# Order of the three products in the split FFN matmuls of a two-block transformer kernel

## The chip, the cores and the metric

One Trainium2 chip, one core of it. The metric is the device time of one execution in microseconds (us), the median of three runs. Engines are named as in the profile: PE is TensorE's matmuls and PEld its weight loads, DVE is VectorE, ACT is ScalarE, POOL is GpSimd, and SP issues most of the DMAs.

## The reference, cut to what matters

The reference runs a hybrid layer and then a two-layer block on 256 tokens of width 1024 (the second block has 256 context tokens beside them). There are five feed-forward networks (FFNs) in it, all of this form, with the inner width 2816:

```
gt, up = jnp.split(h @ w_ffn_in, 2, axis=-1)      # h: [tokens, 1024]; gt and up: [tokens, 2816]
y = (jax.nn.silu(gt) * up) @ w_ffn_out            # [tokens, 1024]
```

The first and the last FFN (numbers 0 and 4 here) work on 256 tokens, the three in between (1 to 3) on 512.

## The kernel before, in words

Weights come from HBM in chunks of up to 2 MB (`wf`) through a ring of three slots. Everything runs in float32, but the FFN matmuls are made from a split: each operand is written as a high part, rounded to a narrower float type (`fp32r`), and a low part, the difference. A product is then the sum of three matmuls: high weight by high activation, high weight by low activation, low weight by high activation. All three add to the same PSUM tile.

An FFN is cut into 34 halves (half a weight chunk each), in three groups of hidden tiles (8, 8 and 6, the table `GROUPS`). In a group come first 8, 8 or 6 "in" halves: each makes two PSUM tiles (gate and up, `c` = 0 and 1) over 8 contraction slices (`k`). Then come 4 "out" halves, each of which makes two tiles of the output over the group's 8, 8 or 6 slices. So a half has 2 x 8 x 3 = 48 matmuls, or 36 in the out halves of the last group, and an FFN has 1584. Moving operands are 256 or 512 columns wide, as the tokens are.

What each engine does for a half `h`:

- ACT, `w_hi(h + 2)` (line 1258), rounds the weights of a later half to `W_hi`; it waits until half `h - 1` has filled its tiles, as there are three buffers. Then it takes silu of the gate tile.
- DVE, `w_lo(h + 2)` (line 1563), subtracts, which makes `W_lo`. Then it multiplies the up tile into silu (line 1672), or adds an out tile to the residual (line 1656).
- POOL, `ffn_parts`, rounds the product to the high activation (line 630, signal `a_hi`) and then makes its low part (line 632, signal `a_lo`).
- In front of an FFN stands a norm: per slice, DVE scales (line 1591), ACT and POOL modulate, ACT makes the high part `z_hi` (line 1296, signal `norm_hi`), DVE the low part `z_lo` (line 1606, signal `norm_lo`). `z_lo` lies in the tensor `zT_r`; all other operands of the split lie in `arena_r`.

PE issues in program order, in `ffn`: lines 801, 802 and 803 are the three products of one slice and tile. It waits for `W_lo` of the half at the half's start. In the first half of an FFN (`i == 0`) the two tiles alternate slice by slice, and slice `k` waits for `norm_lo` of that slice. In the first out half of a group (`second and j == 0`), slice `k` of the first tile waits for `a_lo` of that slice. Every other half runs tile by tile with no wait per slice.

Of the kernel before, what the change touches and what calls it, by code (L numbers as in the profile page):

```python
# [19 lines left out]
P = 128  # L20
# [6 lines left out]
FT = FF // P  # L27
GROUPS = ((0, 8), (8, 8), (16, 6))
# [290 lines left out]
def build(nc, d, out_x):  # L319
# [5 lines left out]
    with ctx:  # L325
# [72 lines left out]
        def sig(name):  # L398
            if name not in sems:
                sems[name] = ctx.enter_context(nc.semaphore(name))  # L400
            return sems[name]
# [126 lines left out]
        def norm_hi_before(q):  # L528
            return KT * sum(1 for p in SPLIT if p < q)
# [145 lines left out]
        def _(pe):  # L675
            mm = nc.tensor.matmul
# [104 lines left out]
            def ffn(f, nt, q):  # L781

                hi, lo = a_parts(nt)
                zh = z_hi(nt)
                for i, (g, j, second) in enumerate(HALVES):
                    h = FFN_HALVES * f + i
                    nk = GROUPS[g][1] if second else KT
                    wh = W_hi[h % NSPLIT][:, 0:nk * 256].rearrange("p (k n) -> p k n", k=nk)
                    wl = W_lo[h % NSPLIT][:, 0:nk * 256].rearrange("p (k n) -> p k n", k=nk)
                    pe.wait_ge(sig("w_lo"), h + 1)  # L790
                    xh, xl = (hi, lo) if second else (zh, z_lo)
                    b = [open_tile(half_first_tile(h) + c) for c in range(2)]

                    for c, k in ([(c, k) for k in range(nk) for c in range(2)] if i == 0 else
                                 [(c, k) for c in range(2) for k in range(nk)]):
                        if i == 0 and c == 0:
                            pe.wait_ge(sig("norm_lo"), norm_hi_before(q) + k + 1)
                        if second and j == 0 and c == 0:
                            pe.wait_ge(sig("a_lo"), FT * f + GROUPS[g][0] + k + 1)
                        whc, wlc = wh[:, k, c * P:(c + 1) * P], wl[:, k, c * P:(c + 1) * P]  # L800
                        mm(b[c][:, 0:nt], whc, xh[:, k, 0:nt], start=(k == 0), stop=False)  # L801
                        mm(b[c][:, 0:nt], whc, xl[:, k, 0:nt], start=False, stop=False)  # L802
                        last = mm(b[c][:, 0:nt], wlc, xh[:, k, 0:nt], start=False, stop=(k == nk - 1))  # L803
                        if k == nk - 1:
                            last.then_inc(filled, 1)

            def merge(br, y, ready):
                for c in range(4):
# [31 lines left out]
            b = open_tile(TILE["strip"])  # L840
            mm(b[0:16, 0:384], K_tbl[0:33, :], oh[0:33, :], start=True, stop=True).then_inc(filled, 1)
            oh = C("oh_fwd")
            b = open_tile(TILE["cbias"])
            for t in range(2):
                for c in range(CMP_N):
                    at = P * t - 16 * c - 31 + 271
                    col = (t * CMP_N + c) * 16
                    last = mm(b[:, col:col + 16], oh[0:33, at:at + P], K_tbl[0:33, :], start=True, stop=True)
# [3 lines left out]
            for k in range(KT):  # L852
                pe.wait_ge(sig("lru_xc"), k + 1)
                for g in range(2):
                    n = TILE["lru_gates"] + 2 * k + g
                    b = open_tile(n)
# [5 lines left out]
            b = open_tile(TILE["gla_lr"])  # L862
            for k in range(KT):
                last = mm(b[0:16, 0:S], wsm[:, k, 48:64], zT[:, k, 0:S], start=(k == 0), stop=(k == KT - 1))
            last.then_inc(filled, 1)
            wait_evac(pe, TILE["gla_lr"])
            for h in range(4):
                b = open_tile(TILE["gla_al"] + h)
# [14 lines left out]
            for t in range(2):  # L883
                b = open_tile(TILE["gla_t"] + t)
                for h in range(4):
                    last = nc.tensor.transpose(b[:, h * P:(h + 1) * P], C_e[:, h, t * P:(t + 1) * P], C("ident"))
                last.then_inc(filled, 1)
            for t in range(2):
                b = open_tile(TILE["gla_att"] + t)
                for h in range(4):  # L890
                    last = mm(b[:, h * P:(h + 1) * P], C_k[:, h, t * P:(t + 1) * P], C_q[:, h, t * P:(t + 1) * P],
                              start=True, stop=True)
# [24 lines left out]
            for h in range(4):  # L917
                for e in range(2):
                    n = TILE["gla_o"] + 2 * h + e
                    b = open_tile(n)  # L920
# [238 lines left out]
            for jp in range(4):  # L1159
                b = open_tile(TILE["ev_mix"] + jp)  # L1160
                for a in range(2):
                    g = 2 * jp + a
# [1049 lines left out]
```

## Time and profile before

| | us |
|---|---|
| median of three runs | 2772.85 |
| lowest and highest | 2766.75, 2776.7 |
| span of the profiled execution | 2777.6 |
| PE busy, in the span | 2601.2 |
| PEld busy | 2035.4 |
| DVE busy | 1053.4 |
| ACT busy | 715.2 |
| POOL busy | 245.8 |

The profiled execution is one of its own; the trace gives its span from the first to the last instruction and no other time for it. It lies 4.75 us (0.17%) above the median of the timed runs. Matmuls overlap in the records, so the duration of one is longer than the distance from its start to the next one's; that distance is what a matmul costs.

### The profile page before, as it was taken

To read this page: it belongs to the slowest core of one execution; us is meant where nothing else is said; L and a number is where in the kernel's file an instruction comes from. 1 tells how busy PE (TensorE), PEld (TensorE's weight loads), DVE (VectorE), ACT (ScalarE), POOL (GpSimd) and SP (SyncE) were. 2 spreads that over 40 slices of the span, in tenths; PEclk is the share of its full clock that TensorE was granted. 3 is DMA by queue.
4 is the path that set the end of the run, shared out by engine and by line. 5 is a ranking of instruction groups with operands and counts; after the bars stand their busy time and mean duration, and the time that the engine had idled before them with its cause. 6 is when DMAs were issued, how large, how long until landed. Compare 5 with 4: busy or idle time off the path is not lost.

```text
span 2777.6 us, 29902 instructions
## 1 busy us (share of the span) xinstructions
PE 2601.2 (94%) x12950; PEld 2035.4 (73%) x12950; DVE 1053.4 (38%) x1289; ACT 715.2 (26%) x1102; POOL 245.8 (9%) x304
## 2 busy tenths in 40 slices
PE   7999999888899899999898989999899999888999
PEld 5757877657799788888444458888688888546899
DVE  1251112361444633333256443333533333255554
ACT  1321001151333421212212332222331222114432
POOL 0000000000011220101100011010120101300110
PEclk8899988879999999999999999999999999998999
DMA  7454423502444432222127522222222222320442
GB/s 309 165 206 187 150 100 136 212 1 91 177 187 177 172 122 91 92 86 96 49 102 289 190 116 91 91 99 94 96 91 91 91 84 97 93 91 31 182 183 92
DMA packets 29106, 354.42 MB, mean 128 GB/s; under 512 B 3330, under 2 KB 5537, under 8 KB 7600
## 3 DMA queue, kind: packets, MB, share of 16 engines
q1 hardware_dynamic: 26272, 343.24, 32.7%
q0 software_dynamic: 2704, 9.28, 1.2%
q8 instruction: 103, 1.69, 0.2%
q14 instruction: 27, 0.22, 0.0%
HBM read 349.53 MB, written 1.13 MB: 126 GB/s over the span
## 4 chain that ended last, share of the span: by engine, by line
PE 88%; DVE 6%; ACT 3%; issue 1%; DMA 1%; POOL 0%; DVEq 0%; SPq 0%; POOLq 0%; ACTq 0%
PE psum L802 18%; PE psum L801 18%; PE psum L803 18%; PE psum L707 12%; PE psum L818 6%; PE psum L716 4%; PE psum L699 2%; PE psum L756 2%; PE psum L1016 1%; PE psum L768 1%; DMA ring<-in_w 1%; PE psum L926 1%; DVE rr L1584 1%; PE psum L728 1%; PE psum L1042 1%
## 5 line engine op out<-in xcount | busy, mean ns | idle before, releaser
L801 PE MATMUL psum<-arena_r 128*128 128x512 f32 (+1 forms) x2640 | 921.1, 349 | 29.8 <-DVE zT_r L1606 29.7
L803 PE MATMUL psum<-arena_r 128*128 128x512 f32 (+1 forms) x2640 | 923.8, 350 | 0.0
L802 PE MATMUL psum<-zT_r,arena_r 128*128 128x512 f32 (+1 forms) x1760 | 621.8, 353 | 0.0
L801 PEld LDWEIGHTS psum<-arena_r 128*128 128x128 f32 x2640 | 502.6, 190 | 101.9 <-issue 32.4
L803 PEld LDWEIGHTS psum<-arena_r 128*128 128x128 f32 x2640 | 501.2, 190 | 64.7
L1258 ACT ACTIVATE arena_r<-ring 128x2048 fp32r<-128x2048 f32 (+1 forms) x170 | 316.8, 1866 | 741.6 <-PE psum L803 732.2
L1563 DVE TENSOR_TENSOR arena_r<-ring,arena_r 128x2048 fp32r<-128x2048 f32 (+1 forms) x170 | 424.6, 2499 | 211.4 <-ACT arena_r L1258 211.3
L802 PEld LDWEIGHTS psum<-zT_r,arena_r 128*128 128x128 f32 x1760 | 334.9, 190 | 46.0
L802 PE MATMUL psum<-arena_r 128*128 128x512 f32 (+1 forms) x880 | 305.0, 347 | 0.0
L707 PE MATMUL psum<-zT,ring 128*128 128x256 f32 (+1 forms) x1040 | 261.7, 413 | 4.2 <-DMA ring<-in_w 2.6
L707 PEld LDWEIGHTS psum<-zT,ring 128*128 128x128 f32 x1040 | 199.6, 193 | 64.2 <-issue 36.3
L802 PEld LDWEIGHTS psum<-arena_r 128*128 128x128 f32 x880 | 166.4, 189 | 20.6
L1656 DVE SCALAR_TENSOR_TENSOR xT<-psum,gates_h,xT 128x256 f32<-128x256 f32 x168 | 74.6, 479 | 194.1 <-PE psum L803 194.1
L1244 ACT ACTIVATE arena<-psum 128x256 f32<-128x256 f32 (+5 forms) x92 | 38.6, 426 | 415.9 <-PE psum L707 284.0
L630 POOL CAST arena_r<-rt 128x512 fp32r<-128x512 f32 (+1 forms) x55 | 29.0, 527 | 1166.9 <-DVE rt L1672 1166.9
L1672 DVE TENSOR_TENSOR rr<-psum,rr 128x512 f32<-128x512 f32 (+1 forms) x55 | 32.2, 585 | 238.6 <-PE psum L803 238.6
L1672 DVE TENSOR_TENSOR rt<-psum,rt 128x512 f32<-128x512 f32 (+1 forms) x55 | 32.1, 584 | 222.2 <-PE psum L803 222.2
L716 PE MATMUL psum<-ring,zT 128*128 128x512 f32 (+1 forms) x288 | 104.3, 522 | 0.0
L818 PE MATMUL psum<-arena,ring 128*128 128x256 f32 x384 | 89.6, 388 | 5.4 <-DVE arena L1826 5.4
L818 PE MATMUL psum<-zT,ring 128*128 128x256 f32 x384 | 89.1, 386 | 0.0
L716 PEld LDWEIGHTS psum<-ring,zT 128*128 128x128 f32 x288 | 49.7, 190 | 53.4 <-issue 53.4
L756 PE MATMUL psum<-ring,cs 128*32 128x512 f32 x576 | 79.6, 683 | 8.3 <-DVE mod L1624 4.2
(256 smaller groups left out, 2169.1 us busy)
## 6 DMA issues: line engine op xcount, KB each, us to landing
ring<-in_w SPq DMA_DIRECT2D x78, 2048.0 KB, 8.6
ring<-in_wf SPq DMA_DIRECT2D x75, 2048.0 KB, 8.4
ring<-in_wf SPq DMA_DIRECT2D x10, 1536.0 KB, 6.6
ring<-in_w SPq DMA_DIRECT2D x2, 1024.0 KB, 5.8
arena<-strip_scratch POOLq DMA_DIRECT2D x1, 2048.0 KB, 22.9
arena<-rpb_scratch POOLq DMA_DIRECT2D x16, 128.0 KB, 11.0
cst<-in_cst SPq DMA_DIRECT2D x1, 1423.0 KB, 26.1
xT<-in_x SPq DMA_DIRECT2D x1, 1024.0 KB, 6.0
```

The costliest lines, as they stand in the source:

```text
L699: last = mm(b[j][:, 0:nt], w[:, k, c:c + P], rhs(k), start=(k == 0), stop=(k == nk - 1))
L707: last = mm(b[:, 0:nt], w[:, k, c:c + P], rhs(k), start=(k == 0), stop=(k == nk - 1))
L716: last = mm(b[:, 0:width], lhs(k, j), w[:, k, c0:c0 + width], start=(k == 0), stop=(k == nk - 1))
L756: last = mm(psum[32 * g:32 * g + 32, at:at + BANK], cs[:, 32 * k:32 * k + 32], w[:, k, :], start=(k < 4), stop=(k >= 4), skip_group_check= ...
L801: mm(b[c][:, 0:nt], whc, xh[:, k, 0:nt], start=(k == 0), stop=False)
L802: mm(b[c][:, 0:nt], whc, xl[:, k, 0:nt], start=False, stop=False)
L803: last = mm(b[c][:, 0:nt], wlc, xh[:, k, 0:nt], start=False, stop=(k == nk - 1))
L818: last = mm(b[:, 0:S], w[:, k, 256 * half + P * j:256 * half + P * j + P], y[:, k, :] if half else zT[:, k, 0:S], start=(k == 0), stop=(k ...
L1258: A(W_hi[h % NSPLIT][:, 0:n], ring[:, at:at + n], ACT.Identity).then_inc(sig("w_hi"), 1)
L1563: v.tensor_tensor(out=W_lo[h % NSPLIT][:, 0:n], in0=ring[:, at:at + n], in1=W_hi[h % NSPLIT][:, 0:n].bitcast(f32), op=ALU.subtract).then_i ...
L1656: last = v.scalar_tensor_tensor(out=xT[:, k, s * S:(s + 1) * S], in0=b[:, s * S:(s + 1) * S], scalar=gate(k, s), in1=xT[:, k, s * S:(s + 1 ...
L1672: v.tensor_tensor(out=a, in0=b[:, 0:nt], in1=a, op=ALU.mult).then_inc(evac["V"], 1)
```

## The change

In each half PE takes the three products in another order. Before, a tile took all three products of slice 0, then all three of slice 1, and so on. Now it takes high by high over all slices, then high weight by low activation over all slices, then low weight by high activation over all slices. In the first half of an FFN the first two of these passes go over both tiles, slice by slice, before either tile gets its third pass. The waits move with the products: the half starts on `w_hi`, and `w_lo` is waited for ahead of the first third pass; the high by high pass waits per slice for `norm_hi` or `a_hi`, and the second pass per slice for `norm_lo` or `a_lo`. Numbers of matmuls, their shapes and all other engines' programs are as they were.

```diff
-                    pe.wait_ge(sig("w_lo"), h + 1)
                     xh, xl = (hi, lo) if second else (zh, z_lo)
                     b = [open_tile(half_first_tile(h) + c) for c in range(2)]
-                    for c, k in ([(c, k) for k in range(nk) for c in range(2)] if i == 0 else
-                                 [(c, k) for c in range(2) for k in range(nk)]):
+                    def hi_hi(c, k):
+                        if i == 0 and c == 0:
+                            pe.wait_ge(sig("norm_hi"), norm_hi_before(q) + k + 1)
+                        if second and j == 0 and c == 0:
+                            pe.wait_ge(sig("a_hi"), FT * f + GROUPS[g][0] + k + 1)
+                        mm(b[c][:, 0:nt], wh[:, k, c * P:(c + 1) * P], xh[:, k, 0:nt], start=(k == 0), stop=False)
+
+                    def hi_lo(c, k):
                         if i == 0 and c == 0:
                             pe.wait_ge(sig("norm_lo"), norm_hi_before(q) + k + 1)
                         if second and j == 0 and c == 0:
                             pe.wait_ge(sig("a_lo"), FT * f + GROUPS[g][0] + k + 1)
-                        whc, wlc = wh[:, k, c * P:(c + 1) * P], wl[:, k, c * P:(c + 1) * P]
-                        mm(b[c][:, 0:nt], whc, xh[:, k, 0:nt], start=(k == 0), stop=False)
-                        mm(b[c][:, 0:nt], whc, xl[:, k, 0:nt], start=False, stop=False)
-                        last = mm(b[c][:, 0:nt], wlc, xh[:, k, 0:nt], start=False, stop=(k == nk - 1))
+                        mm(b[c][:, 0:nt], wh[:, k, c * P:(c + 1) * P], xl[:, k, 0:nt], start=False, stop=False)
+
+                    def lo_hi(c, k):
+                        last = mm(b[c][:, 0:nt], wl[:, k, c * P:(c + 1) * P], xh[:, k, 0:nt],
+                                  start=False, stop=(k == nk - 1))
                         if k == nk - 1:
                             last.then_inc(filled, 1)
+
+                    pe.wait_ge(sig("w_hi"), h + 1)
+                    if i == 0:
+                        for product in (hi_hi, hi_lo):
+                            for k in range(nk):
+                                for c in range(2):
+                                    product(c, k)
+                        pe.wait_ge(sig("w_lo"), h + 1)
+                        for c in range(2):
+                            for k in range(nk):
+                                lo_hi(c, k)
+                        continue
+                    for c in range(2):
+                        for k in range(nk):
+                            hi_hi(c, k)
+                        for k in range(nk):
+                            hi_lo(c, k)
+                        if c == 0:
+                            pe.wait_ge(sig("w_lo"), h + 1)
+                        for k in range(nk):
+                            lo_hi(c, k)
```

## Rows read from the trace of the kernel before

**Rows 1.** The page, part 1: busy time, share of the span, instructions.

```profile
PE 2601.2 (94%) x12950; PEld 2035.4 (73%) x12950; DVE 1053.4 (38%) x1289; ACT 715.2 (26%) x1102; POOL 245.8 (9%) x304
```

**Rows 2.** The page, part 4: the chain that ended last, by line.

```profile
PE psum L802 18%; PE psum L801 18%; PE psum L803 18%; PE psum L707 12%; PE psum L818 6%; PE psum L716 4%; PE psum L699 2%; PE psum L756 2%; PE psum L1016 1%; PE psum L768 1%; DMA ring<-in_w 1%; PE psum L926 1%; DVE rr L1584 1%; PE psum L728 1%; PE psum L1042 1%
```

**Rows 3.** Groups by form: count, busy, mean ns, idle before, releaser.

```profile
L801 PE MATMUL psum<-arena_r 128*128 128x512 f32 x1584 | 621.2, 392 | 22.9 <-DVE zT_r L1606 22.9
```

**Rows 4.** Windows: first matmul of each FFN to its 49th, granted clock behind POOL's.

```profile
751.46:759.60 8.14, 8.14 (x48) 8.14 (x49) 8.11 (x21) 5.32 (x8) 0.00 (x0) 0.67 0.14 28
965.42:978.07 12.65, 12.65 (x49) 10.15 (x50) 11.32 (x16) 10.47 (x16) 6.89 (x5) 0.88 0.04 8
1634.23:1646.88 12.65, 12.65 (x48) 10.21 (x49) 10.21 (x13) 10.63 (x16) 6.89 (x5) 0.87 0.01 3
2012.14:2025.25 13.11, 13.11 (x49) 10.54 (x50) 10.24 (x13) 10.47 (x16) 6.89 (x5) 0.84 0.01 1
2580.46:2588.86 8.40, 8.40 (x48) 8.40 (x49) 5.08 (x13) 8.19 (x15) 0.00 (x0) 0.65 0.55 234
```

**Rows 5.** Timeline: FFN 1's first low part, each FFN's last high part.

```profile
964.42 0.86 DVE L1606 TENSOR_TENSOR zT_r<-zT,arena_r 128x512 fp32r<-128x512 f32 x1 [1.10 <-ACT arena_r L1296]
...
973.34 0.63 ACT L1296 ACTIVATE arena_r<-zT 128x512 fp32r<-128x512 f32 x1
...
754.67 0.42 ACT L1296 ACTIVATE arena_r<-zT 128x256 fp32r<-128x256 f32 x1 [0.31 <-DVE zT L1594]
...
1642.15 0.63 ACT L1296 ACTIVATE arena_r<-zT 128x512 fp32r<-128x512 f32 x1
...
2020.06 0.64 ACT L1296 ACTIVATE arena_r<-zT 128x512 fp32r<-128x512 f32 x1
...
2586.03 0.42 ACT L1296 ACTIVATE arena_r<-zT 128x256 fp32r<-128x256 f32 x1
```

**Rows 6.** Windows: FFN 1's first matmuls, and a stretch of attention.

```profile
965.42:968.44 3.02, 3.02 (x7) 2.44 (x8) 3.02 (x5) 2.13 (x5) 2.46 (x2) 0.50 0.00 0
...
556.00:640.00 84.00, 63.73 (x379) 40.50 (x377) 48.89 (x97) 47.19 (x198) 0.00 (x0) 0.76 0.00 1
```

**Rows 7.** Windows in steady running: in halves, out halves; FFN 2, then FFN 0.

```profile
1657.97:1713.44 55.47, 55.47 (x241) 45.12 (x240) 17.98 (x10) 12.58 (x10) 9.54 (x10) 1.00 0.22 82
1735.45:1768.09 32.64, 32.64 (x146) 27.03 (x144) 12.13 (x15) 5.75 (x3) 0.00 (x0) 1.00 0.34 126
765.30:799.48 34.18, 34.18 (x291) 34.18 (x290) 16.30 (x12) 13.83 (x12) 6.84 (x12) 1.00 0.51 190
805.22:822.50 17.28, 17.28 (x146) 17.28 (x145) 9.15 (x9) 5.74 (x3) 0.00 (x0) 1.00 0.40 137
```

**Rows 8.** Timeline: matmuls in an out half of FFN 1.

```profile
1204.39 0.39 PE L801 MATMUL psum<-arena_r 128*128 128x512 f32 x1
1204.62 0.39 PE L802 MATMUL psum<-arena_r 128*128 128x512 f32 x1
1204.85 0.39 PE L803 MATMUL psum<-arena_r 128*128 128x512 f32 x1
```

**Rows 9.** Timeline: first out halves, starting at 1724.54, 799.48 and 2754.56.

```profile
1725.49 0.61 POOL L630 CAST arena_r<-rr 128x512 fp32r<-128x512 f32 x1 [9.10 <-DVE rr L1672]
1726.18 1.29 POOL L632 TENSOR_TENSOR arena_r<-rr,arena_r 128x512 fp32r<-128x512 f32 x1
1726.74 2.89 DVE L1563 TENSOR_TENSOR arena_r<-ring,arena_r 128x2048 fp32r<-128x2048 f32 x1 [1.32 <-ACT arena_r L1258]
...
800.17 0.40 POOL L630 CAST arena_r<-rr 128x256 fp32r<-128x256 f32 x1 [4.47 <-DVE rr L1672]
...
2755.72 0.75 POOL L632 TENSOR_TENSOR arena_r<-rr,arena_r 128x256 fp32r<-128x256 f32 x1
...
2756.53 0.19 PEld L801 LDWEIGHTS psum<-arena_r 128*128 128x128 f32 x1 [0.22 <-POOL arena_r L632]
...
2756.75 0.28 PE L802 MATMUL psum<-arena_r 128*128 128x256 f32 x1
```

## What I expect of the change

> **What bounds the kernel now.** I read the page's busy times first: PE is busy for 2601.2 of 2777.6 us, no other engine for half of the span, and there are exactly as many weight loads as matmuls, 12950 each [rows 1]. Then the chain that ended last: lines 801 to 803 hold 54% of it [rows 2]. So the split FFN matmuls set the end, and what counts is (a) what one of them costs and (b) how long PE stands still at the FFNs' edges. Idle time in front of the 512-column matmuls of line 801 is 22.9 us in all, all of it put down to `norm_lo` (line 1606) and none to `w_lo` [rows 3]; beyond the FFNs' starts there is almost none to win.
>
> The price of one matmul, from windows in steady running [rows 7]. FFN 2's in halves: 55.47 us for 240 matmuls, 0.2311 us each. Its out halves: 32.64 / 144 = 0.2267. FFN 0's in halves: 34.18 / 288 = 0.1187; out halves: 17.28 / 144 = 0.1200. (The counts of the windows also hold matmuls that only overlap an edge.)
>
> **The first half of each FFN.** Before, slice `k` brings six matmuls of work, so PE works along with the norm and has little left when the last slice arrives. After, a slice brings only two until the last `norm_hi` is there, since the second pass stands behind the first in PE's order. Behind the last slice then lie 34 matmuls: its own 2, and 16 and 16 of the other passes. That the first one can start earlier (on `norm_hi` and not on `norm_lo`) buys nothing, as the last slice decides.
>
> The last high parts end at 973.34 + 0.63 = 973.97, at 1642.78 and 2020.70, and in the 256-column FFNs at 755.09 and 2586.45 [rows 5]. A matmul starts 0.14 after its slice is ready (the low part ended at 964.42 + 0.86 = 965.28 [rows 5], the first matmul came at 965.42 [rows 4]). The 34 take 34 x 0.2311 = 7.86 us, or 34 x 0.1187 = 4.04. The low parts are ready long before pass two needs them. So the second half begins at
>
> - FFN 1: 973.97 + 0.14 + 7.86 = 981.97, against 978.07 [rows 4]: +3.9 us
> - FFN 2: 1650.78 against 1646.88: +3.9
> - FFN 3: 2028.70 against 2025.25: +3.4
> - FFN 0: 755.09 + 0.14 + 4.04 = 759.27 against 759.60: -0.3
> - FFN 4: 2590.63 against 2588.86: +1.8
>
> Together +12.7 us. Nothing behind gives it back: from there to the FFN's end PE is without a gap, so everything shifts.
>
> **The clock in that half.** Each FFN begins at a granted clock of 0.50, which is 1.2 GHz: FFN 1 for its first 3.02 us, seven matmuls [rows 6]; the five first halves ran at means of 0.65 to 0.88 [rows 4]. There PE was working without a pause. After, while it picks up two matmuls per slice, it works 0.86 us (two at 3.02 / 7) in every 1.36 (from 964.42, when the first high part was there, to 973.97 in seven slices [rows 5]), which is 63%. Attention shows such broken work: busy for 63.73 of 84 us it had a mean clock of 0.76 [rows 6], neither always up nor always down. If the clock is up by the last slice, this costs nothing; if it rises only as late after the last slice as it did after the first matmul, some 3 to 6 us of the 34 matmuls run at half speed, 1.5 to 2.5 us lost per FFN, 10 us in all. I take 4, under the middle, as the pairs are nearer to the attention row's three quarters than to none.
>
> The Trainium skill ("TensorE: Matmul & The Clock Gate", the section on HAM oscillation) says that idle gaps between bursts throttle the clock again and advises loops that keep matmuls back to back. It speaks against this change, and by it the sum would take the upper end, 10 us; the rows above leave it open.
>
> **The first out half of a group** (15 of them). Now the wait for the last slice's high part comes after 7 (or 5) matmuls instead of the low part's after 21 (or 15). POOL's rounding of the last slice ends at 1725.49 + 0.61 = 1726.10, 1.56 us after the half began at 1724.54, and in 256 columns at 800.17 + 0.40, 1.09 after 799.48 [rows 9]. After a stall the weight load is exposed: line 632 ended at 2756.47, the load began at 2756.53, the next matmul at 2756.75, 0.22 instead of 0.12 after the one before [rows 9]. So a late slice costs its lateness plus 0.16: effectively ready at 1.73 and 1.25.
>
> - 512 columns: needed at 7 x 0.227 = 1.59, stall 0.14; in the group of six at 1.13, stall 0.60. Three FFNs: 3 x (0.14 + 0.14 + 0.60) = 2.6 us.
> - 256 columns: needed at 0.84, stall 0.41; in the group of six at 0.60, stall 0.65 and 0.10 more for the low part (1.91 + 0.16 against 1.97), of which 0.26 is paid now too (0.22 idle [rows 9] and the load). Two FFNs: 2 x (0.41 + 0.41 + 0.49) = 2.6 us.
>
> The same 0.1 for the last slice of the five first halves: 0.5. Together 5.7 us. For 512 columns the low part is no new wait: 1726.18 + 1.29 is 2.93 after the start, needed at 15 x 0.227 = 3.4. Behind these waits PE alone is queued; the tiles it fills come later, and ACT, DVE and SP's ring with them.
>
> **Waiting for `w_hi` instead of `w_lo`** is worth nothing. DVE makes the low weights two halves ahead: in the half that began at 1724.54 the subtraction for the second half after it ended at 1729.63 [rows 9], 17 us before it is needed. The added waits, when already met, cost nothing: in that half PE passes a wait per slice at its usual pace.
>
> **The price of a matmul in the new order.** Before, the first two of three used the same weights. The trace shows a load for each of them all the same [rows 1], and in out halves the step to a matmul with the same weights (1204.39 to 1204.62) is as long as the next to other weights (1204.62 to 1204.85) [rows 8]. So nothing is lost with the pairing. The skill's same page (Part 2, the step on LDWEIGHTS) says that decoupling lets one load serve many matmuls; if one load served the pair here, breaking it up would cost something. Rows 1 say it is not done here.
>
> But 0.2311 against 0.2267 shows that the price depends on which tensors are streamed: the in halves change between `arena_r` and `zT_r` at two of three matmuls, the out halves never [rows 7]. After, they change twice per tile of 24. If all in halves came to the price of the out halves, 3 x 1056 x 0.0044 = 13.9 us would be won and 2 x 1056 x 0.0013 = 2.7 lost: -11.2. If nothing changes: 0. I take -5, as a third of the in matmuls still stream `zT_r` and each change may need some matmuls to settle. The other bound: every matmul comes to the dearer of its two prices, 1584 x 0.0044 = 7.0 for the out halves in 512 columns and 2112 x 0.0013 = 2.7 for the in halves in 256: +9.7.
>
> **Sum:** 12.7 + 4 + 5.7 - 5 = +17.4 us. Against the profiled span of 2777.6 that is 2795.0; that span lies 4.75 us above the median of the timed runs, so for these 2772.85 + 17.4 = 2790.2.
>
> **Rivals.**
>
> - *Given back in the steady price.* The full 11.2 us are won and the clock costs nothing: 12.7 + 5.7 - 11.2 = +7.2, 2780, within 0.3% (8.3 us, about what a measurement of this kernel can tell). For it: the two prices in rows 7. Against: FFN 0's prices lie the other way round.
> - *Faster: the swap of weights gets hidden.* 512 columns at 2.4 GHz are 213.3 ns, 256 are 106.7; each matmul pays 12 to 18 ns on top. If long passes over one tensor hid this, 4752 x 16.3 ns and 3168 x 12.4 ns, 117 us, would go: about 2675. It decides from 31 us on (8.3 and the 22.4 of the other terms), 3.9 ns per matmul. For it: the surplus isn't the same everywhere. Against: the out halves show three equal steps, be the tensor and the weights the same or not.
> - *Slower by the steady price.* Every matmul comes to the dearer of its prices, +9.7 instead of -5, and the clock costs its full 10: 12.7 + 10 + 5.7 + 9.7 = +38, 2811. For it: each matmul now has other weights than the one before. Against: rows 8.
> - *The change does nothing*, because PE catches up from a reserve: there is none, PE is the bound right behind each of these places.
>
> **Chances.** The forecast's case (+9 to +32) 0.70, given back 0.12, faster 0.10, slower by the steady price 0.08. The likeliest case's own range is 2782 to 2805. With the steady price part of the way to either side, 2777 to 2808 holds eight in ten. Slower by over 0.3%: 0.70 + 0.08 = 0.78, less 0.04 for a sum that is too large by half; within 0.3%: 0.12 + 0.04 = 0.16; faster: 0.10.
>
> **What would show it.** In the timeline of each FFN's start: high by high matmuls in pairs with gaps between them, the 34 matmuls in one run behind the last line 1296, and the second half 3 to 6 us later relative to it in FFNs 1 to 3. In the waits: PE on POOL's rounding (line 630) at all 15 group changes, 0.1 to 0.7 us each, in place of line 632. In windows of in halves: between 0.2267 and 0.2311 per matmul. PEclk in the first halves not above rows 4. The prediction is wrong if the steady price moves by more than 2 ns per matmul, which 7920 of them make 16 us, or if the clock stays low far into the second half.

## The result, and the profile after

The changed kernel takes 2794.71 us (median of four runs, 2790.28 to 2797.97) against 2773.07 for the kernel before (four runs). The ratio is 1.0073, with a 95% interval of 1.0053 to 1.0093. By the ratio that is 20.2 us slower, by the medians 21.6, at a forecast of 17.4 more, and inside the range.

The page of the changed kernel, part 1, and from part 4 the chain by line. Lines 798, 805 and 808 are now the three products (high by high, high by low, low by high).

```profile
PE 2610.4 (94%) x12950; PEld 2034.9 (73%) x12950; DVE 1053.2 (38%) x1289; ACT 714.8 (26%) x1102; POOL 243.2 (9%) x304
...
PE psum L805 18%; PE psum L808 18%; PE psum L798 17%; PE psum L707 12%; PE psum L845 6%; PE psum L716 4%; PE psum L699 2%; PE psum L756 1%; DMA ring<-in_w 1%; PE psum L1043 1%; PE psum L768 1%; POOL zT L614 1%; PE psum L953 1%; DVE rr L1611 1%; PE psum L728 1%
```

The counts are those of [rows 1], and the shares of the three products are within one point of those in [rows 2]; the busy time of no engine but PE moves by more than 3 us. So the chain by line tells nothing here, and the FFNs have to be read in stretches. The best stretch runs from the end of an FFN's last high part (the moment that the norm is done; the change doesn't slow the norm: from the first high part to the last it takes 9.57 us in FFN 1, against 9.59 before, and 6.59 in FFN 4 both times) to the start of its last matmul. First the kernel before, the windows' sum over its five FFNs, then the changed kernel. The first number is the length in us.

```profile
sum 1443.93, PE 1443.91 PEld 1248.07 DVE 568.63 ACT 385.00 POOL 177.98; mean PE 288.78 PEld 249.61 DVE 113.73 ACT 77.00 POOL 35.60
```

```profile
sum 1464.51, PE 1462.15 PEld 1263.79 DVE 568.56 ACT 384.92 POOL 175.61; mean PE 292.43 PEld 252.76 DVE 113.71 ACT 76.98 POOL 35.12
```

The difference is 20.6 us, the measured one is 20.2 (0.0073 of 2773). The spans differ by less (2791.4 - 2777.6 = 13.8), because everything outside these stretches took 1333.7 us in the one profile and 1326.9 in the other, with the same program. That part lies between 1322.4 and 1338.2 us over all profiles of this study (what makes it longer is shown under e1); a span of one profile is no measure for a few us here, the stretches are.

Now the three places. The changed kernel's windows from each FFN's last high part to the start of its second half, in FFNs 0 to 4:

```profile
747.82:754.31 6.49, 6.49 (x36) 6.44 (x35) 5.63 (x11) 3.47 (x4) 0.00 (x0) 0.60 0.39 131
970.15:978.72 8.57, 8.57 (x36) 6.99 (x35) 5.25 (x5) 3.68 (x4) 0.00 (x0) 0.92 0.52 186
1642.43:1651.06 8.63, 8.63 (x35) 7.00 (x35) 2.98 (x2) 3.68 (x3) 0.00 (x0) 0.91 0.00 0
2025.06:2033.54 8.48, 8.48 (x35) 6.89 (x35) 2.98 (x2) 3.68 (x4) 0.00 (x0) 0.93 0.00 0
2594.83:2601.14 6.31, 6.26 (x34) 6.26 (x35) 2.71 (x2) 3.46 (x3) 0.00 (x0) 0.62 0.01 3
sum 38.48, PE 38.43 PEld 33.57 DVE 19.56 ACT 17.98 POOL 0.00; mean PE 7.69 PEld 6.71 DVE 3.91 ACT 3.60 POOL 0.00
```

Before, these were 4.51, 4.10, 4.10, 4.55 and 2.41 us (from [rows 4, 5]), 19.7 in all: 18.8 us more now. The timeline of PE at FFN 1's start shows why: pairs (here those of two slices merged to four matmuls, and in the third row those of three slices to six), a gap until the next high part (line 1323), and only then the run behind the last slice.

```profile
961.79 2.38 PE L798 MATMUL psum<-arena_r 128*128 128x512 f32 x4
964.92 2.38 PE L798 MATMUL psum<-arena_r 128*128 128x512 f32 x4 [0.75 <-ACT arena_r L1323]
967.89 3.53 PE L798 MATMUL psum<-arena_r 128*128 128x512 f32 x6 [0.59 <-ACT arena_r L1323]
971.22 0.54 PE L805 MATMUL psum<-zT_r,arena_r 128*128 128x512 f32 x1
```

The first out half of a group, as windows: a group of eight in FFN 0 and in FFN 2, the group of six in FFN 2; then the weight load that waited in the last one.

```profile
794.26:800.41 6.15, 6.01 (x51) 5.80 (x49) 3.05 (x3) 1.92 (x1) 1.14 (x2) 1.00 0.75 309
1728.34:1739.39 11.05, 11.05 (x50) 8.93 (x48) 4.45 (x4) 1.92 (x1) 1.91 (x2) 1.00 0.05 21
1970.28:1979.10 8.82, 8.49 (x37) 6.62 (x36) 4.34 (x4) 1.49 (x1) 1.91 (x2) 1.00 0.03 9
```

```profile
1971.90 0.19 PEld L798 LDWEIGHTS psum<-arena_r 128*128 128x128 f32 x1 [0.75 <-POOL arena_r L630]
```

The same three halves in the kernel before, as windows:

```profile
799.48:805.22 5.74, 5.74 (x50) 5.74 (x49) 3.05 (x3) 1.92 (x1) 1.14 (x2) 1.00 0.82 331
1724.54:1735.45 10.91, 10.91 (x50) 9.01 (x48) 4.45 (x4) 1.92 (x1) 1.91 (x2) 1.00 0.05 20
1966.91:1975.07 8.16, 8.16 (x37) 6.76 (x36) 4.25 (x4) 1.49 (x1) 1.91 (x2) 1.00 0.04 14
```

Over the 15 halves the sum is 5.4 us more, and line 630 is the releaser, not line 632 as in [rows 9].

The steady price, the counterpart of [rows 7] in the same order, and below it the three passes of one tile in FFN 2 (eight matmuls each: high by high, high by low from `zT_r`, low by high):

```profile
1662.10:1717.30 55.20, 55.20 (x241) 45.06 (x240) 17.96 (x10) 12.57 (x10) 9.51 (x10) 1.00 0.22 83
1739.39:1772.03 32.64, 32.64 (x146) 27.03 (x144) 12.13 (x15) 5.75 (x3) 0.00 (x0) 1.00 0.34 126
760.02:794.26 34.24, 34.24 (x291) 34.24 (x289) 16.31 (x12) 13.81 (x12) 6.81 (x12) 1.00 0.49 185
800.41:817.69 17.28, 17.28 (x147) 17.28 (x145) 9.15 (x9) 5.74 (x3) 0.00 (x0) 1.00 0.38 134
...
1673.14:1674.96 1.82, 1.82 (x10) 1.50 (x9) 0.69 (x1) 1.62 (x1) 0.78 (x2) 1.00 0.00 0
1674.96:1676.83 1.87, 1.87 (x10) 1.50 (x9) 1.54 (x1) 0.30 (x1) 1.12 (x1) 1.00 0.00 0
1676.83:1678.66 1.83, 1.83 (x9) 1.50 (x8) 1.40 (x1) 0.00 (x0) 0.00 (x0) 1.00 0.00 0
```

In these windows in halves of 512 columns went from 0.2311 to 0.2300 us per matmul, those of 256 from 0.1187 to 0.1189; out halves kept 0.2267 and 0.1200 to the digit. Over all steady in halves (63 of 512 columns, 42 of 256) the starts in the two traces give 699.6 us before and 695.5 now, and 239.3 and 239.7: 0.2314 to 0.2300 and 0.1187 to 0.1189, 3.7 us less together. The dear pass is the one from `zT_r` (1.87 / 8 = 0.234), the next one is still settling (0.229). Sum of the three places: 18.8 + 5.4 - 3.7 = 20.5 us, all of the 20.6.

### The profile page after: what moved, and what is told of

It reads as the page before. It is cut to its first block, busy times and chain, and to the rows that moved or that the text cites. A ratio compares the mean times of both kernels' runs of the same rounds, so it can differ in the third digit from the quotient of the medians.

```text
span 2791.4 us, 29902 instructions
## 1 busy us (share of the span) xinstructions
PE 2610.4 (94%) x12950; PEld 2034.9 (73%) x12950; DVE 1053.2 (38%) x1289; ACT 714.8 (26%) x1102; POOL 243.2 (9%) x304
## 4 chain that ended last, share of the span: by engine, by line
PE 87%; DVE 6%; ACT 3%; DMA 2%; issue 2%; POOL 1%; DVEq 0%; SPq 0%; POOLq 0%; ACTq 0%
PE psum L805 18%; PE psum L808 18%; PE psum L798 17%; PE psum L707 12%; PE psum L845 6%; PE psum L716 4%; PE psum L699 2%; PE psum L756 1%; DMA ring<-in_w 1%; PE psum L1043 1%; PE psum L768 1%; POOL zT L614 1%; PE psum L953 1%; DVE rr L1611 1%; PE psum L728 1%
## 5 line engine op out<-in xcount | busy, mean ns | idle before, releaser
L798 PE MATMUL psum<-arena_r 128*128 128x512 f32 (+1 forms) x2640 | 567.3, 355 | 33.2 <-ACT arena_r L1323 30.0
L808 PE MATMUL psum<-arena_r 128*128 128x512 f32 (+1 forms) x2640 | 543.2, 348 | 0.0
L798 PEld LDWEIGHTS psum<-arena_r 128*128 128x128 f32 x2640 | 440.5, 193 | 116.9 <-issue 28.9
L808 PEld LDWEIGHTS psum<-arena_r 128*128 128x128 f32 x2640 | 433.7, 189 | 66.4
L805 PE MATMUL psum<-zT_r,arena_r 128*128 128x512 f32 (+1 forms) x1760 | 368.5, 353 | 0.0
L805 PEld LDWEIGHTS psum<-zT_r,arena_r 128*128 128x128 f32 x1760 | 291.6, 191 | 46.9
L805 PE MATMUL psum<-arena_r 128*128 128x512 f32 (+1 forms) x880 | 181.8, 347 | 0.0
L805 PEld LDWEIGHTS psum<-arena_r 128*128 128x128 f32 x880 | 144.9, 189 | 20.9
L845 PEld LDWEIGHTS psum<-arena,ring 128*128 128x128 f32 x384 | 74.1, 193 | 15.1 <-issue 4.7
```

The source lines that it names most:

```text
L798: mm(b[c][:, 0:nt], wh[:, k, c * P:(c + 1) * P], xh[:, k, 0:nt], start=(k == 0), stop=False)
L805: mm(b[c][:, 0:nt], wh[:, k, c * P:(c + 1) * P], xl[:, k, 0:nt], start=False, stop=False)
L808: last = mm(b[c][:, 0:nt], wl[:, k, c * P:(c + 1) * P], xh[:, k, 0:nt], start=False, stop=(k == nk - 1))
L845: last = mm(b[:, 0:S], w[:, k, 256 * half + P * j:256 * half + P * j + P], y[:, k, :] if half else zT[:, k, 0:S], start=(k == 0), stop=(k ...
```

## The experiments

Each kernel ran beside the kernel before on its chip; the ratio is to that. All medians and ratios:

| run | median us | before, there | ratio (95%) | stretches, sum us |
|---|---|---|---|---|
| before | 2773.07 | | | 1443.9 |
| changed | 2794.71 | 2773.07 | 1.0073 (1.0053 to 1.0093) | 1464.5 |
| e1_first_half_old | 2782.68 | 2774.63 | 1.0025 (1.0010 to 1.0041) | 1446.1 |
| e2_group_old | 2790.71 | 2774.63 | 1.0065 (1.0043 to 1.0088) | 1459.6 |
| e3_both_old | 2775.39 | 2774.63 | 1.0002 (0.9990 to 1.0014) | 1441.0 |
| e4_fillers | 2787.85 | 2774.63 | 1.0053 (1.0034 to 1.0072) | 1458.9 |
| e5_no_low_part | 2760.17 (one run) | 2775.76 | | 1433.0 |
| e6_arena_moved | 2763.76 | 2775.76 | 0.9956 (0.9944 to 0.9969) | 1434.1 |
| e7_zT_moved | 2766.54 | 2775.76 | 0.9967 (0.9956 to 0.9978) | 1434.0 |
| e8_high_first | 2766.45 | 2775.76 | 0.9966 (0.9954 to 0.9979) | 1436.3 |
| e9_both | 2763.61 | 2773.90 | 0.9966 (0.9953 to 0.9978) | 1432.2 |
| e10_128_bytes | 2764.72 | 2773.90 | 0.9970 (0.9958 to 0.9982) | 1438.2 |
| e11_256_bytes | 2765.25 | 2773.90 | 0.9970 (0.9959 to 0.9982) | 1436.5 |
| e12_old_steady | 2763.78 | 2774.41 | 0.9958 (0.9944 to 0.9973) | 1430.0 |

**e1_first_half_old**

```diff
                     if i == 0:
-                        for product in (hi_hi, hi_lo):
-                            for k in range(nk):
-                                for c in range(2):
-                                    product(c, k)
                         pe.wait_ge(sig("w_lo"), h + 1)
-                        for c in range(2):
-                            for k in range(nk):
-                                lo_hi(c, k)
+                        for k in range(nk):
+                            pe.wait_ge(sig("norm_lo"), norm_hi_before(q) + k + 1)
+                            for c in range(2):
+                                hi_hi(c, k)
+                                hi_lo(c, k)
+                                lo_hi(c, k)
```

> The changed kernel with the first half of each FFN back in the old order (six matmuls per slice, waiting for the low part); all other halves stay changed. Theory: the first halves cost 18.8 us (second halves begin 2.0, 4.5, 4.5, 3.9 and 3.9 us later behind the last high part than before), so this run should take about 2794.7 - 18.8 = 2776 us, within 0.3% of the kernel before, with the five first halves back at 8.1 to 13.1 us each. Rival, that the loss sits in the waits for the activations at the group changes or in the steady price: about 2790 to 2795, the first halves back but the end not.

2782.68 us, 12 less than the changed kernel, where 18.8 were expected. The windows' sum over the stretches of this run:

```profile
sum 1446.13, PE 1443.81 PEld 1248.41 DVE 569.50 ACT 384.72 POOL 175.56; mean PE 288.76 PEld 249.68 DVE 113.90 ACT 76.94 POOL 35.11
```

18.4 us of the 20.6 are back in the stretches. The timed ratio (6.9 us above before, interval 2.8 to 11.4) doesn't reach down to the 2.2 that the stretches leave; the profile has its surplus outside them, 1338.2 us, the most of all runs, in a program that is the same there. Two parts of that program show where it comes from, the one up to FFN 0 and the one between FFNs 1 and 2, first in this run and then in the changed kernel:

```profile
0.00:751.76 751.76, 681.67 (x3182) 522.88 (x3183) 201.60 (x373) 160.18 (x442) 9.64 (x20) 0.88 0.41 158
1333.00:1641.27 308.27, 267.28 (x1131) 131.36 (x1129) 134.80 (x218) 70.25 (x158) 11.57 (x14) 0.92 0.42 161
```

```profile
0.00:743.51 743.51, 671.88 (x3182) 517.43 (x3183) 200.62 (x371) 159.56 (x441) 9.64 (x20) 0.90 0.42 160
1330.97:1633.18 302.21, 260.22 (x1131) 126.01 (x1129) 133.63 (x217) 69.35 (x157) 11.56 (x14) 0.94 0.43 164
```

The same work took 8.2 and 6.1 us more (0.7 us of each because the FFN's first matmul waits for the low part here) at a lower granted clock (0.88 for 0.90, 0.92 for 0.94). The second part took 308.2 us in e3 too. The timed executions of e1 vary in the same way, from 2773.7 us at a mean granted clock of 0.953 to 2788.0 at 0.945. So the first halves are the loss's main part by the stretches; the 4.7 us between ratio and stretches are of the size of what the clock does elsewhere, and whether this order brings that about or chance does, no run shows.

**e2_group_old**

```diff
+                    if second and j == 0:
+                        pe.wait_ge(sig("w_lo"), h + 1)
+                        for c in range(2):
+                            for k in range(nk):
+                                if c == 0:
+                                    pe.wait_ge(sig("a_lo"), FT * f + GROUPS[g][0] + k + 1)
+                                hi_hi(c, k)
+                                hi_lo(c, k)
+                                lo_hi(c, k)
+                        continue
```

> The changed kernel with the first out half of each of the 15 groups back in the old order, waiting for the low part slice by slice. Theory: these halves took 5.4 us more in the changed kernel (12.30 against 11.50 us for two of them in FFN 0, 22.10 against 21.78 in FFNs 1 to 3, 5.04 against 4.57 and 8.8 against 8.16 for the groups of six), so about 2794.7 - 5.4 = 2789 us, and no idle time of PE on line 630. Rival, that a stall there is made good later: the same time as the changed kernel, 2795.

2790.71, 4 us less than the changed kernel by the medians, which the intervals of the two ratios can't tell from nothing. The trace can: the halves in question are back at 5.76, 10.88 and 8.16 us, and the stretches sum to 1459.6, 4.9 less (5.4 less in these halves, 0.6 more in the first halves, where the clock rose at other moments). A stall at the group change is not made good later.

**e3_both_old** has both edits.

> Both places back in the old order, all other halves in the new one. Theory: what is left of the change is the steady price alone, which fell from 231.1 to 230.0 ns in the 512-column in halves and rose from 118.7 to 118.9 in the 256-column ones: 3.7 us less than before, 2769 us, a ratio near 0.9987 to the kernel before. Rival, that the new order costs something that the first halves hide (evacuations at other moments, later ring refills): 2773 or more.

The time is that of the kernel before, 1.0002 (0.9990 to 1.0014); expected was 0.9987, just outside. In the stretches 2.9 us are won:

```profile
sum 1440.99, PE 1440.99 PEld 1248.69 DVE 568.18 ACT 384.81 POOL 177.62; mean PE 288.20 PEld 249.74 DVE 113.64 ACT 76.96 POOL 35.52
```

So the steady gain is there in the trace, and too small for the timed runs to show. With both places undone the loss is gone, in time as in the stretches, which is what this run had to show.

**e4_fillers**

```diff
                     if i == 0:
+                        for k in range(nk):
+                            for c in range(2):
+                                hi_hi(c, k)
+                            if k < nk - 1:
+                                for r in range(2):
+                                    mm(psum[:, 4 * BANK:4 * BANK + nt], wh[:, 0, 0:P],
+                                       W_hi[h % NSPLIT][:, 0:nt], start=True, stop=True)
```

(the second and third pass as in the changed kernel)

> The changed kernel, but in the first half of each FFN two matmuls into an unused PSUM bank, whose result nobody reads, follow each pair of the first pass (14 in all per FFN), so that PE works through the norm nearly without a pause. Theory: of the 18.8 us of the first halves about 6 are the low clock (it rose 5.2 and 4.8 us after the last high part in FFNs 0 and 4, about 1.2 us after it in FFNs 1 to 3); with the fillers it rises before the last high part, and the run takes about 2789 us; behind the last high part lie 8.0 us to the second half in FFNs 1 to 3 and 4.2 in FFNs 0 and 4. Rival, that broken work and not the count of matmuls behind the last slice is all of the loss: the second halves come as early as before, 2776. Rival, that the clock does not depend on the pauses: no gain, 2795, or slightly more as PE falls behind the norm.

2787.85 us, 7 less than the changed kernel with 70 matmuls more (the intervals of the two ratios overlap, so what follows rests on the traces). The windows from the last high part to the second half, FFNs 0, 1 and 4:

```profile
747.30:751.93 4.63, 4.63 (x42) 4.63 (x40) 4.59 (x11) 3.48 (x3) 0.00 (x0) 1.00 0.24 50
967.80:975.79 7.99, 7.99 (x35) 6.49 (x35) 5.25 (x5) 3.69 (x4) 0.00 (x0) 1.00 0.52 179
...
2591.41:2595.59 4.18, 4.13 (x34) 4.13 (x35) 2.72 (x2) 3.47 (x3) 0.00 (x0) 1.00 0.00 0
sum 32.80, PE 32.75 PEld 28.25 DVE 18.54 ACT 18.01 POOL 0.00; mean PE 6.55 PEld 5.65 DVE 3.71 ACT 3.60 POOL 0.00
```

The granted clock is 1.00 in all of them, where the changed kernel had 0.60, 0.92 and 0.62, and the lengths fall to the 8.0 and 4.2 us that 34 matmuls take. That splits the 18.8 us: 38.48 - 32.80 = 5.7 us are the clock, 32.80 - 19.68 = 13.1 the matmuls that wait behind the last slice. Neither rival holds. The clock's part changes from one execution to the next: with the same first halves as the changed kernel, e2 had 39.05 us in these windows, and with those of the kernel before, e1, e3 and e5 had 20.0 to 20.4.

**e5_no_low_part** (one run) leaves the product with the low part of the activation out of the in halves.

```diff
-                    xh, xl = (hi, lo) if second else (zh, z_lo)
+                    xh, xl = (hi, lo) if second else (zh, zh)
```

> The kernel before, but in the in halves the second product streams the high part again in place of z_lo, so that these halves never read zT_r; the product with the low part of the activation is left out of the result. Theory: the surplus price of the in halves (231.1 against 226.7 ns in 512 columns, 118.7 against 120.0 in 256) belongs to streaming from zT_r, so the in halves come to 226.7 and 120.0. Rival, that it belongs to the in halves for another reason (the tiles' evacuations by ACT and DVE, the place of z_hi in the arena): 231.1 and 118.7 stay.

The windows of the in halves of FFN 2 (240 matmuls) and FFN 0 (288):

```profile
1646.07:1700.47 54.40, 54.40 (x241) 45.06 (x240) 17.97 (x10) 12.57 (x10) 9.53 (x10) 1.00 0.22 84
...
757.22:791.78 34.56, 34.56 (x291) 34.56 (x289) 16.30 (x12) 13.81 (x12) 6.85 (x12) 1.00 0.52 189
```

0.2267 and 0.1200, the prices of the out halves exactly. Streaming from `zT_r` is what makes an in half's price. How it does so shows in the changed kernel, by the starts over all its in halves of 512 columns: the eight steps of a pass from `z_hi` take 226.7 ns on average, those from `zT_r` 233.7, and those of the third pass 229.7. If only the streamed tensor counted, the three would average 229.0. The changed order has 230.0, as its third pass starts dear, and the order of before, which goes to `zT_r` and back at every slice, 231.4. So a part of the price is in the changes between the tensors, and the new order saved more than half of that part.

**e6_arena_moved** and **e7_zT_moved**, on the kernel before (e7 has a pad in front of `zT` too):

```diff
+        sb("pad", 8)
         arena_at = nc.sbuf_base
```

> The kernel before with 32 unused bytes per partition in front of the arena, nothing else. zT begins at byte 32896 of a partition and the arena at 129184, which is 32 off a multiple of 64; now both begin at multiples of 64. Theory: zT_r's price comes from where it lies in relation to the weights in the arena, so in halves and out halves now have one price, 226.7 and 120.0, which is 11 us less, about 2763 us. Rival, that the place of the streamed operand alone sets the price: everything gets zT_r's price, about 233.6 and 118.6, which is 2 x 1.1 + 7 us and more, about 2785. Second rival, that addresses of 32 bytes don't matter: 231.1, 226.7 and the time of before.

> As the run before, but with 32 bytes in front of zT and 32 more in front of the arena: both begin 32 off a multiple of 64, as the arena alone does in the kernel before. If the relation of the two sets the price: 226.7 and 120.0 everywhere and about 2763 us, as there. If the place of the streamed operand alone sets it: 226.7 and 120.0 here too, unlike there. If addresses don't matter: as before, 2774.

Both are faster, 0.9956 and 0.9967. The windows of the in halves, FFN 2 and FFN 0, in e6 and then in e7:

```profile
1643.51:1698.44 54.93, 54.93 (x242) 45.12 (x240) 18.02 (x10) 12.58 (x10) 9.57 (x10) 1.00 0.22 84
...
754.35:788.27 33.92, 33.92 (x291) 33.92 (x290) 16.30 (x12) 13.81 (x12) 6.82 (x12) 1.00 0.53 193
```

```profile
1650.03:1704.96 54.93, 54.93 (x241) 45.07 (x240) 17.96 (x10) 12.57 (x10) 9.50 (x10) 1.00 0.22 83
...
760.88:794.80 33.92, 33.92 (x291) 33.92 (x289) 16.31 (x12) 13.81 (x12) 6.83 (x12) 1.00 0.52 192
```

0.2289 and 0.1178, the same in both, though `zT` and the arena begin 32 bytes further on in e7 than in e6 and only the distance from `zT` to the arena is the same (96320 bytes; 96288 in the kernel before). So the distance sets the price and the place alone doesn't. (The weights and `z_hi` both lie in the arena and moved together; the runs don't tell which of the two distances counts.) But the theory that an equal offset to multiples of 64 would give the out halves' price fell: 0.2267 and 0.1200 were expected. The time came out right (2763.76) in part by luck: the steady in halves won 7.4 us in 512 columns where 13.9 were expected, and 1.8 in 256 columns where 2.7 were to be lost, and the stretches as a whole won 9.8.

**e8_high_first** keeps the changed order in steady halves. In the first half of an FFN it has, per slice:

```diff
+                        for k in range(nk):
+                            for c in range(2):
+                                hi_hi(c, k)
+                                mm(b[c][:, 0:nt], wl[:, k, c * P:(c + 1) * P], xh[:, k, 0:nt], start=False, stop=False)
+                            for c in range(2):
+                                last = hi_lo(c, k, stop=(k == nk - 1))
```

and the same order per slice in the first out half of a group.

> The changed order in all steady halves; in the first half of each FFN and the first out half of each group the order is slice by slice, as before, but within a slice high by high, then low weight by high activation, and only then high weight by low activation, each with its own wait. Theory: PE starts on the high part, 0.5 to 0.9 us earlier per FFN than before, and still has six matmuls per slice, so behind the last high part lie 3.2 to 3.8 us in FFNs 0 to 3 and 2 in FFN 4; 3.7 us less from that, 3.7 less from the steady price, 0.5 less from the group changes: 2767 us, ratio 0.9972. Rival, that the waits for the low part then stall PE in between: first halves as long as before, 2770.

2766.45 us, 0.9966. The windows from the last high part to the second half:

```profile
747.89:752.06 4.17, 4.17 (x31) 4.17 (x29) 4.14 (x11) 3.08 (x2) 0.00 (x0) 0.78 0.20 39
966.42:970.11 3.69, 3.69 (x17) 3.00 (x16) 3.66 (x5) 3.12 (x3) 0.00 (x0) 1.00 0.02 4
...
2571.12:2572.36 1.24, 1.24 (x12) 1.24 (x12) 0.43 (x1) 1.24 (x1) 0.00 (x0) 1.00 0.00 0
sum 16.25, PE 16.25 PEld 14.23 DVE 13.07 ACT 13.71 POOL 0.00; mean PE 3.25 PEld 2.85 DVE 2.61 ACT 2.74 POOL 0.00
```

3.4 us less than before in these, and no stall on the low part. The profiles scatter here with the clock, but without overlap: with the order of before in the first halves these windows sum to 18.6 to 20.4 us (before, e1, e3, e5, e6, e7), with the high products first to 15.0 to 16.4 (e8 to e12). Waiting for the high part alone is worth something, if the slice keeps all its work.

**e9_both, e10_128_bytes, e11_256_bytes** are e8 with the arena moved by 32, 128 and 256 bytes.

> The version with the high products first and the changed order in steady halves, and the arena moved by 32 bytes. The first starts bring 3.7 us and the group changes 0.5 as they did alone (behind the last high part 4.2, 3.7, 3.7, 3.5 and 1.3 us). The steady price: with the distance from zT_r to the arena 32 bytes longer, the old order had 228.9 and 117.8 ns in the in halves and 226.7 and 120.0 in the out halves, 9.8 us less over the five FFNs. If the price belongs to each streamed tensor at this distance, passes of eight from the arena cost 226.7 and those from zT_r less than 233.6, the mean is again near 228.9, and the gains add up: 2775.8 - 9.8 - 4 = 2762 us, ratio 0.995. Rival, that the gain of the moved arena and that of the new order are the same gain: 2766.

> The same order with the arena moved by 128 bytes. The two moved runs had one price (228.9 and 117.8) at the same distance between zT and the arena, with the tensors themselves at other places, so the distance and not the place sets it, but not through multiples of 64 alone, as this was neither zT_r's price nor that of the out halves. If the price is a matter of the distance in small steps, the passes from zT_r have a third price here, and the others stay at 226.7. If it was only the odd 32 bytes: 233.6 as in the changed kernel, since 128 keeps them.

> The same with the arena moved by 256 bytes, which keeps the odd 32 bytes too. Distance in small steps: a price of its own again. Only the odd 32 bytes: 233.6 for the passes from zT_r, and 118.6 in 256 columns, as in the changed kernel and as with 128 bytes; the time then is that of the unmoved version, 2766 us.

The pass from `zT_r` (eight matmuls) as windows, FFN 2 and then FFN 4: moved by 32, by 128 and by 256 bytes.

```profile
1661.15:1663.02 1.87, 1.87 (x10) 1.50 (x8) 1.53 (x1) 0.31 (x1) 1.16 (x1) 1.00 0.00 0
...
2585.90:2586.83 0.93, 0.93 (x11) 0.93 (x9) 0.00 (x0) 0.93 (x1) 0.85 (x2) 1.00 0.72 299
```

```profile
1660.15:1662.03 1.88, 1.88 (x10) 1.51 (x8) 1.53 (x1) 0.31 (x1) 1.12 (x1) 1.00 0.00 0
...
2586.01:2586.97 0.96, 0.96 (x10) 0.96 (x9) 0.00 (x0) 0.96 (x1) 0.87 (x2) 1.00 1.07 461
```

```profile
1661.37:1663.24 1.87, 1.87 (x9) 1.50 (x8) 1.53 (x1) 0.31 (x1) 1.13 (x1) 1.00 0.00 0
...
2586.34:2587.29 0.95, 0.95 (x10) 0.95 (x9) 0.00 (x0) 0.95 (x1) 0.87 (x2) 1.00 0.69 293
```

256 bytes give the unmoved kernel's figures back (its in halves: 55.20 us for 240 matmuls and 34.24 for 288, both as in the changed kernel); 32 and 128 each have their own (55.13 and 33.92; 55.33 and 34.40). So it is neither steps of 64 nor the odd 32 bytes alone. The figures fit a price that repeats every 256 bytes of distance: in the arena every streamed slice lies a multiple of 512 bytes from every slice of the weights, at 226.7 and 120.0 ns, and `zT_r` lies 32 bytes off a multiple of 256 in the kernel before, 64 off in e9 and 160 off in e10. The run that would test this, with `zT` at an exact multiple of 256, was not made. The gains of order and layout only partly add up: the stretches fall to 1432.2 with both, and the timed ratio is 0.9966 (0.9953 to 0.9978), where 0.995 was expected, and no better than either alone.

**e12_old_steady** goes back to the order of before in all steady halves, and keeps e9's layout and its starts.

> The old order in all steady halves, the arena moved by 32 bytes, and at the FFNs' starts and group changes the high products first. With the moved arena the old steady order cost 228.9 ns against 229.7 of the new one in the 512-column in halves and the same 117.8 in 256 columns, so 2.5 us less than the version that has both; the FFN stretches from the last high part on should add up to 1430 us (1434.1 with the moved arena alone, 1432.2 with both), and the time to about 2761, ratio 0.994 to 0.996. Rival, that the two kinds of gain don't add up in the time as they did not in the version with both: 2764, ratio 0.9960.

```profile
sum 1429.98, PE 1429.98 PEld 1241.57 DVE 568.96 ACT 384.38 POOL 180.59; mean PE 286.00 PEld 248.31 DVE 113.79 ACT 76.88 POOL 36.12
```

The stretches come to the 1430 that was expected, 13.9 us less than before, the least of all. The time is 2763.78, ratio 0.9958 (0.9944 to 0.9973). It beats both kernels of this case; it can't be told from e6 to e11 by its time.

## Why the prediction was right, step by step

- *The matmuls behind the last slice*: forecast 12.7 us and 0.5 for the exposed loads; 13.1 by e4. Right in place and size, and for each of the five FFNs within 0.3 us.
- *The clock in the first half*: forecast 4 us of at most 10, measured 5.7 by e4. The term was too small, and its split was another: FFNs 0 and 4 lost 1.9 and 2.1 us, FFNs 1 to 3 only 0.5 to 0.6 each. I had spread it evenly. In FFNs 0 and 4 the clock rose 5.2 and 4.8 us after the last high part, as late as the prediction's worst case, and in FFNs 1 to 3 after 1.2 to 1.5 us. The busy share of the pairs doesn't explain this: a pair fills 0.43 us of 0.94 in FFN 4 and of 0.73 in FFN 0 (46 and 59%), and 0.86 of 1.36 in 512 columns (63%), so FFN 0 is nearer to FFNs 1 to 3 in that; but its norm ends 4.5 us after the first high part, theirs after 9.4 to 9.6. What decides, no run shows. The advice of the Trainium skill ("TensorE: Matmul & The Clock Gate", the section on HAM oscillation) to keep matmuls back to back agrees with e4. The 10 us that the prediction took from it don't: that section is on waits for DMAs that are far longer than the pauses here, which the timeline above has at 0.59 and 0.75 us.
- *The group changes*: forecast 5.3, measured 5.4, and each kind of half to 0.1 us. The wait is on line 630, as said.
- *`w_hi` in place of `w_lo`*: no difference seen, as forecast; nothing of PE's waits was on either.
- *The steady price*: forecast -5 of a range from -11.2 to +9.7, measured -3.7. The -5 was a choice between the bounds and not worked out, so that it came close is luck in part. Out halves did not move at all, though no two neighbours share weights any more; so the pairing was worth nothing, as [rows 8] said. The mechanism as forecast (a third of the in matmuls stays dear, and a change of tensor takes some matmuls to settle) is shown by e5 and by the three passes.
- *The rivals*: given back would have wanted -11.2 at the steady price; the swap of weights wasn't hidden (out halves 0.2267); the dear prices did not spread. PE had no reserve.
- *The sum*: 17.4 against 20.2 by the ratio, 20.6 in the stretches and 21.6 by the medians; against the stretches, of the 3 us missing, 1.7 are the clock and 1.3 the steady price.

## What to carry to other kernels

When a consumer starts on slices while they are still being made, keep all the work of a slice together: what is put off until the last slice has come stands bare at the end. If an order is to be changed for a wait, change it inside the slice (the product that needs the late operand last), which here won 3.4 us in the first halves where the pass order lost 18.8. And measure a matmul's price from start to start in each kind of stretch; a difference of 1 ns, times 7920, is 8 us here.

## What the runs showed of the hardware

- The step from one matmul of this kind to the next changed with how far the streamed tensor and the arena, which holds the weights and `z_hi`, lie apart in a partition: with 96288 bytes, 234 ns in a pass from `zT_r` of 512 columns and 119 of 256 (1.87 / 8 and 0.95 / 8); with 32 bytes more 234 and 116; with 128 more 235 and 120; with 256 more as with none. The steady out halves, streamed from the weights' own tensor, had 226.7 and 120.0 in every run. After a pass from `zT_r` of 512 columns five steps still differ (230, 236, 228, 232 and 231 ns in the changed kernel, by the starts over all in halves), then they are at 226.7; the first step of the pass from `zT_r` itself is dear at once (234). What lies behind it wasn't found.
- 32 unused bytes made the whole kernel 0.44% faster (0.31% to 0.56%) in e6; with the same distance at other places, in e7, it was 0.33% (0.22% to 0.44%).
- The granted clock at the FFNs' starts followed the pauses: 0.56 in the changed kernel's first halves of FFNs 0 and 4, 0.81 and 0.78 with fillers that do nothing else. With the fillers it was up before the last high part in all five FFNs, in the changed kernel in none.
- The same program outside the FFNs' stretches took between 1322.4 and 1338.2 us over the fourteen profiles; in the longest (e1) the two parts shown ran at a lower granted clock (0.88 and 0.92) than in the changed kernel (0.90 and 0.94).
